# Expert weights in half-size transfers: eight half buffers, one per step, in place of four buffers of two steps

## The chip, the cores and the metric

The kernel runs on one core of one Trainium2 chip. The metric is device time in microseconds (us) of one execution. Everything is computed in float32. SBUF has 128 partitions; weights come from HBM by DMA over the core's 16 DMA engines.

## What is computed

The reference is two model blocks in a row on 256 tokens of width 1024. The first block has two layers, each a hybrid mixer (HGRN, attention, SSM) and then a PEER layer: for each token, 8 heads choose 16 of 16,384 experts each, and every expert is one row `down` and one row `up` of 1024 numbers. The second block has an RG-LRU layer and a sparse attention layer, each with an MLP.

Only the PEER layers are touched by the change. In short, with `h` the normed tokens:

```
scores  = top 16 of (sub_key_1 . q1 + sub_key_2 . q2)      per head
gate    = softmax(scores)
y[t]    = sum over chosen e of gate[t, e] * gelu(h[t] . down[e]) * up[e]
x       = x + y
```

## The kernel before, in words

The PEER layer splits the tokens. The first 160 (`DT_TOK`) go the dense way: TensorE computes `h . down[e]` for all experts, one step for each 128 experts, and later multiplies by all the `up` rows; non-chosen experts have a gate of zero. The other 96 tokens go the sparse way: GpSimd gathers the rows of their chosen experts (`PAIR`, 96 tiles of 128 rows, 8 KB a row, 1 MB a tile, four buffers, `GBUF`), and VectorE works them off, a dot product (`dot`, L1561) and a weighted sum (`weigh`, L1574) for each. GpSimd issues gather j when `weigh(j - 4)` is done (L975).

The dense way has 128 `hidden` steps (L740 to L750) and then 128 `back` steps (L766 to L777) on TensorE. One step multiplies eight 128x128 weight tiles, 512 KB, with the 160 tokens. Each float32 matmul is two instructions, so a step is 16 matmul instructions. In HBM two steps' weights lie side by side: a row of `experts` is 8 KB for a partition, 4 KB for each step (`pairs`, L1970).

SyncE brings the weights, one transfer of 1 MB for two steps (L362), into `ring`, four buffers of 8 KB a partition (`RING`, `buffer_of`). A buffer is handed back after its second step: by `hidden_ready` (one for each step, SyncE waits for every second one, L359) or by `step_used` (which TensorE raises after every odd `back` step, L776). SyncE issues in order, and TensorE waits for the buffer's semaphore `step_loaded` at each step. There are 128 such transfers in a layer, 256 in all.

Other work is laid by hand between the steps. 20 times in the second half of the `hidden` steps and 20 times in the first half of the `back` steps, after each third step, TensorE makes the gate matrices (`gates`, L762, 16 instructions); VectorE prepares the one-hots, multiplies the gates into the activations (`keep`, L1692) and then does `TILES_AT[n]` gather tiles. When the last `keep` is done, VectorE does the remaining tiles back to back while TensorE goes on with `back` steps from the 60th to the 128th. After step 120 TensorE waits until all 96 tiles are added (`pair_added`) and folds them in (L808, L809). At the end of each section SyncE clears the semaphores before the other engines go on (L380 to L382). Two MLPs use the same ring with transfers of their own (`stream`), which the change leaves alone.

Of the kernel before, what the change touches and what calls it, by code (L numbers as in the profile page):

```python
# [31 lines left out]
NKEYS = 128  # L32
# [4 lines left out]
RING = 4  # L37
# [23 lines left out]
PAIRS = NKEYS  # L61
# [4 lines left out]
def slot_of(section, b):  # L66
    return SLOT_ORDER[section][b % SLOTS]
# [6 lines left out]
    return earlier + b // SLOTS + 1  # L74


def buffer_of(layer, i):
    return (i + 2 * layer) % RING


class Chain:
# [17 lines left out]
def program(nc, I, out):  # L99
    ctx = ExitStack()  # L100
    with ctx:
        def sb(n, s, d=F32):
            return ctx.enter_context(nc.sbuf_tensor(n, s, d))

        ring = sb("weight_ring", [P, SLOTS * SLOT])
# [152 lines left out]
            "xs_turned xs_ready cum_rows decay_exponent decay_ready decayed_scores ssm_product z_silu ssm_mean ssm_root "  # L258
            "mix_turned mix_T key_scores scores_copied"
        ).split()  # L260
        stream_names = "step_loaded0 step_loaded1 step_loaded2 step_loaded3 step_used hidden_ready stream_added dve_chain".split()
        peer_names = (
            "gate_bent gate_exp_ready choice_ready choice_turned choice_T "
            "onehots_ready gates_product hidden_kept gated routing_done pack_ready "
# [9 lines left out]
        S = {n: ctx.enter_context(nc.semaphore(n)) for n in names}  # L274
# [29 lines left out]
        def _(sp):  # L304
            def block(n, b, load):

                s = slot_of(n, b)
                sp.dma_start(ring[:, s * SLOT:(s + 1) * SLOT], load(b)).then_inc(block_loaded[s], 16)
# [8 lines left out]
            def clear(group):  # L317
                for name in group:
                    sp.sem_clear(S[name])
# [30 lines left out]
            def peer(l, load, ahead):  # L350

                last_in_slot = {slot_of(l, b): b for b in range(HYBRID_BLOCKS)}
                for i in range(PAIRS):
                    r = buffer_of(l, i)
                    if i < RING:

                        sp.wait_ge(S["proj_done"], 2 * last_in_slot[r // 2] + 2)
                    elif i < PAIRS // 2 + RING:
                        sp.wait_ge(S["hidden_ready"], 2 * (i - RING + 1))  # L359
                    else:  # L360
                        sp.wait_ge(S["step_used"], i - RING + 1 - PAIRS // 2)
                    sp.dma_start(ring[:, r * 2048:(r + 1) * 2048], load(i)).then_inc(S[f"step_loaded{r}"], 16)  # L362
                    if i == PAIRS // 2 + 16:

                        sp.wait_ge(S["hidden_kept"], NKEYS + 2)
                        sp.wait_ge(S["gated"], GROUPS)
                        clear(front_names[:len(front_names) // 2])
                    if i == PAIRS // 2 + 20:
                        clear(front_names[len(front_names) // 2:])

                sp.wait_ge(S["gated"], 2 * GROUPS)
                for b in range(SLOTS):
                    if b:
                        sp.wait_ge(S["step_used"], PAIRS // 2 - 4 + 2 * b)
                    block(l + 1, b, ahead)

            def section_clear(n, group):
# [42 lines left out]
        def _(pe):  # L420
# [316 lines left out]
            def peer(l):  # L737
                gate_bank = lambda n: bank[(2, 3, 4)[n % 3] if n < GROUPS else (2, 3, 0)[n % 3]]

                def hidden(s):  # L740

                    i, r = s // 2, buffer_of(l, s // 2)
                    pe.wait_ge(S[f"step_loaded{r}"], 16 * (i // RING + 1))

                    pe.wait_ge(S["hidden_kept"], s + 1)
                    w = ring[:, r * 2048 + (s % 2) * 1024:r * 2048 + (s % 2 + 1) * 1024]
                    for k in range(KD):
                        last = mm(bank[s % 2][:, 0:DT_TOK], w[:, k * P:(k + 1) * P], HT[:, k, 0:DT_TOK],  # L748
                                  start=k == 0, stop=k == KD - 1)
                    last.then_inc(S["hidden_ready"], 1)  # L750

                def gates(n):

                    pe.wait_ge(S["onehots_ready"], n + 1)
                    if n >= 3:

                        pe.wait_ge(S["gated"], n - 2)
                    if n >= GROUPS:

                        pe.wait_ge(S["hidden_kept"], NKEYS + 2)  # L760
                    for j in range(8):
                        last = mm(gate_bank(n)[:, j * HALF:(j + 1) * HALF], OH1[:, n % 2, j, :], OH2[:, n % 2, j, :],  # L762
                                  start=True, stop=True)
                    last.then_inc(S["gates_product"], 1)

                def back(s):  # L766

                    i = NKEYS // 2 + s // 2
                    r = buffer_of(l, i)
                    pe.wait_ge(S[f"step_loaded{r}"], 16 * (i // RING + 1))  # L770
                    w = ring[:, r * 2048 + (s % 2) * 1024:r * 2048 + (s % 2 + 1) * 1024]
                    for k in range(KD):
                        last = mm(bank[4 + k // 2][:, (k % 2) * DT_TOK:(k % 2 + 1) * DT_TOK], w[:, k * P:(k + 1) * P], HACT[:, s, :],  # L773
                                  start=s == 0 and k % 2 == 0, stop=s == NKEYS - 1, skip_group_check=True)
                    if s % 2:
                        last.then_inc(S["step_used"], 1)  # L776
                    return last  # L777

                for s in range(CHOICE_AT):
                    hidden(s)  # L780
                pe.wait_ge(S["choice_ready"], 6)
                for w, src in enumerate((N1, N2, TS)):
                    turn(bank[2 + w][:, 0:P], src[:, 0, :, :].rearrange("p a b -> p (a b)"))
                    turn(bank[2 + w][:, P:DT_TOK], src[0:DT_TOK - P, 1, :, :].rearrange("p a b -> p (a b)"),
                         DT_TOK - P).then_inc(S["choice_turned"], 1)
                for s in range(CHOICE_AT, HALF):
                    hidden(s)
                n = 0
                for s in range(HALF, NKEYS):
                    hidden(s)  # L790
                    if s - HALF in HIDDEN_GATE_AT:
                        gates(n)
                        n += 1

                pe.wait_ge(S["gated"], GROUPS)
                for s in range(HALF):
                    back(s)
                    if s in GATE_AT:
                        gates(n)
                        n += 1  # L800
                pe.wait_ge(S["gated"], 2 * GROUPS)
                for s in range(HALF, NKEYS):
                    back(s)
                    if s == NKEYS - 8:

                        pe.wait_ge(S["pair_added"], TILES)
                        for q in range(2):
                            mm(bank[2 + q][GT0 - P:P, :], fold[:, 0:64], ACC[:, 0, q * 512:(q + 1) * 512], start=True, stop=True)  # L808
                            mm(bank[2 + q][GT1 - P:GT0 - P, :], fold[:, 64:96], ACC[:, 1, q * 512:(q + 1) * 512], start=True, stop=True)  # L809
                pe.wait_ge(S["step_used"], PAIRS // 2)  # L810
                pe.sem_inc(S["down_done"], 1)

                pe.wait_ge(S["down_copied"], 4)
                for k in range(KD):
                    last = turn(bank[k // 4][:, (k % 4) * P:(k % 4 + 1) * P], OT[:, k, 0:P])
                last.then_inc(S["back_turned"], 1)
                for k in range(KD):
                    last = turn(bank[2 + k // 4][0:DT_TOK - P, (k % 4) * P:(k % 4 + 1) * P], OT[:, k, P:DT_TOK])
                last.then_inc(S["back_turned"], 1)
# [11 lines left out]
            w = blk(3)  # L831
            for n in range(4):

                pe.wait_ge(S["conv_done"], n + 1)
                for j in range(2):
# [3 lines left out]
                    for g in range(2):  # L839
                        for k in range(2):  # L840
                            last = mm(bank[c % 4][:, g * T:(g + 1) * T],
                                      w[:, 2 * n + k, g * 256 + j * P:g * 256 + (j + 1) * P], XR[:, 2 * n + k, :],
                                      start=k == 0, stop=k == 1)
# [15 lines left out]
            for b in (3, 4):  # L859
                w = blk(b)  # L860
# [4 lines left out]
                for g in range(NG):  # L865

                    for half in range(2):
                        for k in range(KD):
                            last = mm(bank[4 + 2 * (b % 2) + g // 2][64 * half:64 * half + 64, (g % 2) * T:(g % 2 + 1) * T],  # L869
                                      w[:, k, g * HD:(g + 1) * HD], HT[:, k, :], start=k == 0, stop=k == KD - 1)  # L870
# [9 lines left out]
            for w in range(2):  # L880
                for r in range(32):
                    for half in range(2):
                        p0 = 64 * half
                        last = mm(bank[2 * w + half][0:64, 0:45].rearrange("p (c n) -> p c n", n=NC), w1[p0:p0 + 64, w, r, :],
                                  ZC[p0:p0 + 64, w, :, r:r + 16 * (NC - 1) + 1:16], start=r == 0, stop=r == 31)
# [8 lines left out]
            for x in range(4):  # L894
                last = mm(bank[5][0:NC, x * HD:(x + 1) * HD], HID[0:64, 1, x // 2, (x % 2) * NC:(x % 2 + 1) * NC], W2[0:64, 1, :],
                          start=True, stop=True)
# [1107 lines left out]
```

## Time and profile before

| | us |
|---|---|
| median of 3 runs | 2658.49 |
| lowest, highest | 2653.73, 2660.36 |
| the profiled execution, its own time | 2662.17 |
| its span | 2660.4 |
| TensorE busy in it | 2572.5 (97%) |
| VectorE busy in it | 1322.6 (50%) |

The profile's page gives busy time, then the span in 40 slices of 66.5 us. In the slices, one digit is the busy share in tenths. The two PEER layers' dense steps lie from 255 to 903 us and from 1143 to 1790 us. Times in the trace are from the span's start. "PE" is TensorE's matmul, "PEld" its weight load, "q1" the DMA queue of SyncE, "q0" that of GpSimd's gathers, "q10" that of ScalarE.

### The profile page before, as it was taken

The page shows a single profiled execution, that of the slowest core. Times are in us where ns is not written, and L with a number is a line of the kernel's source. Part 1 is how long each engine was busy: PE and PEld are TensorE (multiplying, and loading weights), DVE is VectorE, ACT ScalarE, POOL GpSimd, SP SyncE. Part 2 cuts the span into 40 slices and gives each one's busy share as a digit, 9 for nine tenths or more (in the row PEclk, how much of TensorE's full clock was granted, in tenths as well). Part 3 has the DMA queues.
Part 4 walks back from the last instruction along what each step waited for, and adds up shares of the span by engine and source line. Part 5 has one row for each costly group of instructions (what it writes and reads, how often), then busy time and mean ns, then how long its engine had stood idle before and what let it go on. Part 6 is the DMA issues. An engine that isn't in the chain of part 4 may idle for free.

```text
span 2660.4 us, 36834 instructions
## 1 busy us (share of the span) xinstructions
PE 2572.5 (97%) x15426; PEld 2167.1 (81%) x15426; DVE 1322.6 (50%) x2597; ACT 407.4 (15%) x1166; POOL 211.0 (8%) x208
## 2 busy tenths in 40 slices
PE   6999999999999999999999999999999999999998
PEld 5557999999999865699999999888666677776665
DVE  3843786888853185178687886414400010541001
ACT  2121121111110122022211111003100000430000
POOL 0000111222211000001121221100000000000000
PEclk9999999999999999999999999999999999889999
DMA  5213798999999532159899999973244442003442
GB/s 204 102 64 113 267 381 321 392 395 409 417 420 385 186 127 95 64 209 374 305 386 397 402 412 419 421 278 126 101 154 146 152 153 105 1 1 127 151 149 95
DMA packets 84758, 625.38 MB, mean 235 GB/s; under 512 B 10443, under 2 KB 12978, under 8 KB 14206
## 3 DMA queue, kind: packets, MB, share of 16 engines
q1 hardware_dynamic: 55580, 420.85, 41.3%
q0 software_dynamic: 28032, 201.54, 18.6%
q8 instruction: 113, 1.85, 0.3%
q10 hardware_dynamic: 994, 0.82, 0.1%
q14 instruction: 39, 0.32, 0.0%
HBM read 621.91 MB, written 1.06 MB: 234 GB/s over the span
## 4 chain that ended last, share of the span: by engine, by line
PE 86%; DVE 6%; DMA 5%; ACT 1%; issue 1%; SPq 0%; DVEq 0%; PEldq 0%; ACTq 0%
PE bank L748 17%; PE bank L773 17%; PE bank L499 9%; PE bank L513 8%; PE bank L521 8%; PE bank L762 5%; DMA weight_ring<-in_experts 5%; PE bank L464 4%; PE bank L476 3%; PE bank L869 2%; PE bank L426 1%; PE bank L918 1%; PE bank L488 1%; PE bank L430 1%; PE bank L937 1%
## 5 line engine op out<-in xcount | busy, mean ns | idle before, releaser
L773 PE MATMUL bank<-arena,weight_ring 128*128 128x160 f32 x4096 | 573.6, 301 | 10.7 <-DMA weight_ring<-in_experts 10.6
L773 PEld LDWEIGHTS bank<-arena,weight_ring 128*128 128x128 f32 x4096 | 558.6, 190 | 19.1 <-DMA weight_ring<-in_experts 17.4
L748 PE MATMUL bank<-hidden_T,weight_ring 128*128 128x160 f32 x4096 | 569.0, 301 | 5.1 <-ACT arena L1100 5.1
L748 PEld LDWEIGHTS bank<-hidden_T,weight_ring 128*128 128x128 f32 x4096 | 559.7, 191 | 6.1 <-issue 5.9
L1561 DVE CUSTOM_DVE_ANT_0 arena<-arena 128x1024 f32<-128x1024 f32 x192 | 234.7, 1222 | 168.4 <-DMA arena<-in_expert_rows,choice_by_pair 167.8
L976 POOL DMA_INDIRECT arena<-in_expert_rows,choice_by_pair x192 | 203.8, 1062 | 831.2 <-DVE arena L1574 786.3
L499 PE MATMUL bank<-hidden_T,weight_ring 128*128 128x256 f32 (+1 forms) x1088 | 241.9, 383 | 14.1 <-DMA weight_ring<-in_dense_h 7.4
L499 PEld LDWEIGHTS bank<-hidden_T,weight_ring 128*128 128x128 f32 (+1 forms) x1088 | 203.2, 188 | 47.1 <-issue 8.9
L1574 DVE SCALAR_TENSOR_TENSOR arena<-arena,pair_weights 128x1024 f32<-128x1024 f32 x188 | 240.8, 1281 | 0.2
L513 PEld LDWEIGHTS bank<-hidden_T,weight_ring 128*128 128x128 f32 x1024 | 195.0, 190 | 52.5 <-issue 29.6
L513 PE MATMUL bank<-hidden_T,weight_ring 128*128 128x256 f32 x1024 | 231.2, 380 | 0.0
L1718 DVE TENSOR_TENSOR weight_ring<-weight_ring 128x256 f32<-128x256 f32 x64 | 27.2, 425 | 409.1 <-ACT weight_ring L1146 409.1
L521 PE MATMUL bank<-weight_ring 128*128 128x512 f32 x512 | 229.9, 593 | 0.0
L521 PEld LDWEIGHTS bank<-weight_ring 128*128 128x128 f32 x512 | 97.5, 190 | 95.8 <-issue 92.6
L762 PE MATMUL bank<-weight_ring 128*128 128x64 f32 x1280 | 151.6, 272 | 0.0
L1100 ACT ACTIVATE arena<-bank 128x160 f32<-128x160 f32 x256 | 77.4, 303 | 484.3 <-PE bank L748 484.2
L762 PEld LDWEIGHTS bank<-weight_ring 128*128 128x128 f32 x1280 | 151.2, 192 | 0.0
L464 PE MATMUL bank<-weight_ring,hidden_T 128*128 128x512 f32 (+1 forms) x288 | 120.9, 574 | 0.0
L1106 ACT ACTIVATE pair_weights<-pair_dots 128x1 f32<-128x1 f32 x192 | 38.4, 200 | 508.3 <-DVE pair_dots L1561 508.2
L1680 DVE TENSOR_TENSOR weight_ring<-iota_row,weight_ring 128x1024 f32<-128x1024 f32 x80 | 97.5, 1219 | 8.9 <-ACT weight_ring L1122 8.9
L464 PEld LDWEIGHTS bank<-weight_ring,hidden_T 128*128 128x128 f32 x288 | 52.2, 195 | 57.0 <-issue 56.6
L1692 DVE TENSOR_TENSOR arena<-arena,bank 128x512 f32<-128x512 f32 x80 | 54.8, 685 | 78.5 <-PE bank L762 78.5
(320 smaller groups left out, 2007.4 us busy)
## 6 DMA issues: line engine op xcount, KB each, us to landing
weight_ring<-in_experts SPq DMA_DIRECT2D x256, 1024.0 KB, 8.9
weight_ring<-in_mlp SPq DMA_DIRECT2D x64, 1024.0 KB, 4.8
weight_ring<-in_dense_h SPq DMA_DIRECT2D x22, 2048.0 KB, 7.7
weight_ring<-in_dense_nsa SPq DMA_DIRECT2D x9, 2048.0 KB, 7.7
weight_ring<-in_dense_rg SPq DMA_DIRECT2D x7, 2048.0 KB, 7.9
arena<-in_expert_rows,choice_by_pair POOLq DMA_INDIRECT x192, 10.9
arena<-distance_bias_scratch SPq DMA_DIRECT2D x2, 768.0 KB, 5.7
residual<-in_x SPq DMA_DIRECT2D x1, 1024.0 KB
```

Source lines behind the costliest of these rows:

```text
L464: last = mm(bank[4 + 2 * (b % 2) + tt][:, 0:n], src[:, k, tt * P:(tt + 1) * P], w[:, k, 0:n], start=k == 0, stop=k == KD - 1)
L476: last = mm(bank[4 + 2 * ((first + c) % 2) + tt][:], HT[:, k, tt * P:(tt + 1) * P], w[c][:, k, :], start=k == 0, stop=k == KD - 1)
L499: last = mm(bank[4 + 2 * (b % 2) + j // 2][0:m, (j % 2) * T:(j % 2 + 1) * T], w[:, k, j * P:j * P + m], HT[:, k, :], start=k == 0, stop=k ...
L513: last = mm(bank[r % 2][:, 0:T], ring[:, r * 2048 + k * P:r * 2048 + (k + 1) * P], HT[:, k, :], start=k == 0, stop=k == KD - 1)
L521: last = mm(outs[o][:], act_c[:, r, (o // 2) * P:(o // 2 + 1) * P], ring[:, r * 2048 + 1024 + (o % 2) * 512:r * 2048 + 1024 + (o % 2 + 1) ...
L748: last = mm(bank[s % 2][:, 0:DT_TOK], w[:, k * P:(k + 1) * P], HT[:, k, 0:DT_TOK], start=k == 0, stop=k == KD - 1)
L762: last = mm(gate_bank(n)[:, j * HALF:(j + 1) * HALF], OH1[:, n % 2, j, :], OH2[:, n % 2, j, :], start=True, stop=True)
L773: last = mm(bank[4 + k // 2][:, (k % 2) * DT_TOK:(k % 2 + 1) * DT_TOK], w[:, k * P:(k + 1) * P], HACT[:, s, :], start=s == 0 and k % 2 == ...
L976: pool.indirect_dma_start(PAIR[:, j % GBUF, :], None, I["expert_rows"], bass.IndirectOffsetOnAxis(ap=picked[:, 0, j:j + 1].bitcast(U32), a ...
L1561: V.tensor_tensor_reduce(out=rows, in0=rows, in1=GX[:, j // TILES0, :], scale=1.0, scalar=0.0, op0=ALU.mult, op1=ALU.add, accum_out=adot[: ...
L1574: V.scalar_tensor_tensor(acc, rows, c, acc, ALU.mult, ALU.add).then_inc(S["pair_added"], 1)
L1680: V.tensor_tensor(OH1[:, n % 2, :, :], bc(iota[:].unsqueeze(1), [P, 8, P]), bc(it[:, 0], [P, 8, P]), ALU.is_equal)
```

## The change

Each 1 MB transfer becomes two of 512 KB, one for each step. The ring becomes eight half buffers of 4 KB a partition (`half_of`), each with its own semaphore; the memory is the same. The source of a transfer is one half of the 8 KB row, so a partition gets 4 KB in one piece. Each half is handed back by its own step: SyncE waits for every single `hidden_ready`, and TensorE raises `step_used` after every `back` step. SyncE issues 256 transfers in a layer in place of 128. The section clears have four semaphores more. The places where SyncE clears names between the transfers and where it begins the next section's blocks are the same, counted in steps. Matmuls, VectorE, ScalarE and GpSimd are unchanged.

```diff
-def buffer_of(layer, i):
-    return (i + 2 * layer) % RING
+def half_of(layer, h):
+    return (h + 4 * layer) % (2 * RING)
...
-                for i in range(PAIRS):
-                    r = buffer_of(l, i)
-                    if i < RING:
-
-                        sp.wait_ge(S["proj_done"], 2 * last_in_slot[r // 2] + 2)
-                    elif i < PAIRS // 2 + RING:
-                        sp.wait_ge(S["hidden_ready"], 2 * (i - RING + 1))
+                for h in range(2 * PAIRS):
+                    r = half_of(l, h)
+                    if h < 2 * RING:
+
+                        sp.wait_ge(S["proj_done"], 2 * last_in_slot[r // 4] + 2)
+                    elif h < NKEYS + 2 * RING:
+                        sp.wait_ge(S["hidden_ready"], h - 2 * RING + 1)
                     else:
-                        sp.wait_ge(S["step_used"], i - RING + 1 - PAIRS // 2)
-                    sp.dma_start(ring[:, r * 2048:(r + 1) * 2048], load(i)).then_inc(S[f"step_loaded{r}"], 16)
-                    if i == PAIRS // 2 + 16:
+                        sp.wait_ge(S["step_used"], h - 2 * RING + 1 - NKEYS)
+                    sp.dma_start(ring[:, r * 1024:(r + 1) * 1024], load(h // 2)[:, (h % 2) * 1024:(h % 2 + 1) * 1024]).then_inc(
+                        S[f"step_loaded{r}"], 16)
+                    if h == NKEYS + 32:
...
                 def back(s):
 
-                    i = NKEYS // 2 + s // 2
-                    r = buffer_of(l, i)
-                    pe.wait_ge(S[f"step_loaded{r}"], 16 * (i // RING + 1))
-                    w = ring[:, r * 2048 + (s % 2) * 1024:r * 2048 + (s % 2 + 1) * 1024]
+                    r = half_of(l, NKEYS + s)
+                    pe.wait_ge(S[f"step_loaded{r}"], 16 * ((NKEYS + s) // (2 * RING) + 1))
+                    w = ring[:, r * 1024:(r + 1) * 1024]
...
-                    if s % 2:
-                        last.then_inc(S["step_used"], 1)
+                    last.then_inc(S["step_used"], 1)
```

## Rows read from the trace of the kernel before

**Rows 1.** The page, part 2: the span in 40 slices.

```profile
PE   6999999999999999999999999999999999999998
DMA  5213798999999532159899999973244442003442
```

**Rows 2.** Stretches, both layers: columns as the second line names them.

```profile
core 0: us, PE busy (x) PEld busy (x) DVE busy (x) ACT busy (x) POOL busy (x), PEclk, DMA share, GB/s
580.00:739.00 159.00, 159.00 (x1229) 159.00 (x1228) 134.30 (x173) 16.41 (x66) 35.09 (x33) 1.00 1.01 411
739.00:846.00 107.00, 101.86 (x723) 98.25 (x722) 53.26 (x68) 10.95 (x44) 18.73 (x20) 1.00 1.01 420
846.00:883.00 37.00, 37.00 (x272) 36.89 (x272) 3.52 (x4) 0.50 (x2) 0.00 (x0) 1.00 0.73 263
```

**Rows 3.** Groups by line, 739 to 846 us, then PEld from 1626 to 1740 us.

```profile
L773 PEld LDWEIGHTS bank<-arena,weight_ring 128*128 128x128 f32 x721 | 98.4, 190 | 8.8 <-DMA weight_ring<-in_experts 8.8
L1561 DVE CUSTOM_DVE_ANT_0 arena<-arena 128x1024 f32<-128x1024 f32 x23 | 28.2, 1226 | 56.3 <-DMA arena<-in_expert_rows,choice_by_pair 56.3
L1574 DVE SCALAR_TENSOR_TENSOR arena<-arena,pair_weights 128x1024 f32<-128x1024 f32 x22 | 28.2, 1281 | 0.0
...
L773 PEld LDWEIGHTS bank<-arena,weight_ring 128*128 128x128 f32 x771 | 105.1, 190 | 8.7 <-DMA weight_ring<-in_experts 8.7
```

**Rows 4.** Timeline: start us, us, what, idle before.

```profile
796.05 1.23 DVE L1561 CUSTOM_DVE_ANT_0 arena<-arena 128x1024 f32<-128x1024 f32 x1 [2.53 <-DMA arena<-in_expert_rows,choice_by_pair]
796.11 4.37 PEld L773 LDWEIGHTS bank<-arena,weight_ring 128*128 128x128 f32 x32 [0.57 <-DMA weight_ring<-in_experts]
...
798.75 0.94 POOL L976 DMA_INDIRECT arena<-in_expert_rows,choice_by_pair  x1 [4.02 <-DVE arena L1574]
801.02 1.23 DVE L1561 CUSTOM_DVE_ANT_0 arena<-arena 128x1024 f32<-128x1024 f32 x1 [2.54 <-DMA arena<-in_expert_rows,choice_by_pair]
801.09 4.37 PEld L773 LDWEIGHTS bank<-arena,weight_ring 128*128 128x128 f32 x32 [0.61 <-DMA weight_ring<-in_experts]
```

**Rows 5.** DMA by queue (packets, MB, share), 739 to 846 us, and issues to landing.

```profile
q1 hardware_dynamic: 3123, 22.78, 51.1%
q0 software_dynamic: 3045, 22.12, 49.8%
...
weight_ring<-in_experts SPq DMA_DIRECT2D x23, 1024.0 KB, 14.9
arena<-in_expert_rows,choice_by_pair POOLq DMA_INDIRECT x20, 12.2
```

**Rows 6.** The same view, 580 to 739 us.

```profile
weight_ring<-in_experts SPq DMA_DIRECT2D x28, 1024.0 KB, 9.3
arena<-in_expert_rows,choice_by_pair POOLq DMA_INDIRECT x33, 10.6
```

**Rows 7.** DMA by queue in the start-up: 5.0 to 5.5, then 6.5 to 7.0 us.

```profile
q10 hardware_dynamic: 29, 0.06, 70.3%
q1 hardware_dynamic: 29, 0.04, 28.1%
...
q10 hardware_dynamic: 57, 0.10, 51.8%
q1 hardware_dynamic: 58, 0.03, 19.6%
```

**Rows 8.** DMA by queue, 2657 to 2659 us: the output alone.

```profile
q1 hardware_dynamic: 199, 0.82, 101.9%
```

**Rows 9.** Landing, 260 to 335 us (L976), and SyncE's issues, 739 to 846 us.

```profile
DMA to landing us min/median/max: 5.9/11.8/17.3
...
L362 SPq DMA_DIRECT2D weight_ring<-in_experts x23: 327/328/328, 741.4 to 845.6; - x23
```

**Rows 10.** Timeline at the section's end, and the chain's first `hidden` steps.

```profile
909.04 1.13 PE L430 MATMUL bank<-identity 128*128 128x128 f32 x8 [3.49 <-SPq L382]
...
255.42 82.80 PE bank L748 x608
```

**Rows 11.** A stretch in which TensorE often stands, just after the section's end.

```profile
903.00:912.00 9.00, 4.93 (x42) 4.59 (x43) 3.40 (x9) 3.35 (x7) 0.00 (x0) 1.00 0.84 281
20.00:40.00 20.00, 12.62 (x64) 11.02 (x63) 4.87 (x9) 1.17 (x3) 0.00 (x0) 0.83 0.94 355
```

More of the change, by code:

```diff
@@ L260, in program @@
         ).split()
-        stream_names = "step_loaded0 step_loaded1 step_loaded2 step_loaded3 step_used hidden_ready stream_added dve_chain".split()
+        stream_names = "step_loaded0 step_loaded1 step_loaded2 step_loaded3 step_loaded4 step_loaded5 step_loaded6 step_loaded7 step_used hidden_ready stream_added dve_chain".split()
         peer_names = (
@@ L367, in peer @@
                         clear(front_names[:len(front_names) // 2])
-                    if i == PAIRS // 2 + 20:
+                    if h == NKEYS + 40:
                         clear(front_names[len(front_names) // 2:])
@@ L373, in peer @@
                     if b:
-                        sp.wait_ge(S["step_used"], PAIRS // 2 - 4 + 2 * b)
+                        sp.wait_ge(S["step_used"], NKEYS - 8 + 4 * b)
                     block(l + 1, b, ahead)
@@ L740, in hidden @@
                 def hidden(s):
-                    i, r = s // 2, buffer_of(l, s // 2)
-                    pe.wait_ge(S[f"step_loaded{r}"], 16 * (i // RING + 1))
+                    r = half_of(l, s)
+                    pe.wait_ge(S[f"step_loaded{r}"], 16 * (s // (2 * RING) + 1))
                     pe.wait_ge(S["hidden_kept"], s + 1)
-                    w = ring[:, r * 2048 + (s % 2) * 1024:r * 2048 + (s % 2 + 1) * 1024]
+                    w = ring[:, r * 1024:(r + 1) * 1024]
                     for k in range(KD):
@@ L766, in back @@
                 def back(s):
-                    i = NKEYS // 2 + s // 2
-                    r = buffer_of(l, i)
-                    pe.wait_ge(S[f"step_loaded{r}"], 16 * (i // RING + 1))
-                    w = ring[:, r * 2048 + (s % 2) * 1024:r * 2048 + (s % 2 + 1) * 1024]
+                    r = half_of(l, NKEYS + s)
+                    pe.wait_ge(S[f"step_loaded{r}"], 16 * ((NKEYS + s) // (2 * RING) + 1))
+                    w = ring[:, r * 1024:(r + 1) * 1024]
                     for k in range(KD):
@@ L809, in peer @@
                             mm(bank[2 + q][GT1 - P:GT0 - P, :], fold[:, 64:96], ACC[:, 1, q * 512:(q + 1) * 512], start=True, stop=True)
-                pe.wait_ge(S["step_used"], PAIRS // 2)
+                pe.wait_ge(S["step_used"], NKEYS)
                 pe.sem_inc(S["down_done"], 1)
```

## The prediction, made before the change was run

> **What bounds the kernel now.** I read the slices first: TensorE is busy nearly everywhere, and DMA is at nine tenths or more in two long stretches, the PEER layers [rows 1]. So TensorE sets the time, and DMA is the resource that can stop it. Then the PEER layer by stretches: while gates are made (580 to 739 us) TensorE never stands, though DMA runs at 411 GB/s; from 739 to 846 us its weight loads are busy 98.25 of 107 us, at 420 GB/s; after 846 us it is full again and DMA has room [rows 2]. The groups say what is missing: 8.8 us of idle time before the weight loads of L773 for want of `in_experts`, and 8.7 us in the other layer [rows 3]. These 17.5 us are all that better weight delivery could give. TensorE needs 82.80 / 38 = 2.18 us for a step of 512 KB (608 instructions are 38 steps) [rows 10], so it wants 240 GB/s.
>
> Why only there? In this tail VectorE takes gather tiles back to back. It works 1.23 + 1.28 = 2.51 us on one and would take 417 GB/s by itself; it waits 56.3 us for gathers [rows 3]. Both streams are hungry, and the timeline shows what comes of it: a tile and a pair of steps start every 4.97 us, in step with each other (796.05 to 801.02, 796.11 to 801.09) [rows 4]. In 4.97 us one transfer of 1 MB of each kind lands: 210 GB/s each, 22.78 against 22.12 MB [rows 5]. A step then comes every 2.49 us where 2.18 are wanted.
>
> **How the two queues share.** The whole case hangs on this. Weights take 14.9 us to land and gathers 12.2 [rows 5], so 14.9 / 4.97 = 3.0 weight transfers and 2.5 gathers are under way. Yet both get the same bandwidth. A single line served in order of arrival would give weights 3.0 of 5.5 parts and both the same delay. So each queue gets a turn, whatever waits behind it. What is a turn: a piece (the packet of the rows, one partition's run) or an equal amount of bytes? In the tail it can't be seen, since all pieces are 8 KB. The start-up shows two queues with unequal pieces: 29 packets against 29, then 57 against 58, while the bytes are 0.10 against 0.03 MB [rows 7]. The turn went by packets there. I take it to hold here too.
>
> The Trainium skill ("DMA: Bandwidth & Descriptors", Queues, rings and completion order) says that each DMA engine goes round its queues a packet at a time, a packet being some 9 to 17 descriptors. The start-up's equal counts agree with turns; how many pieces make one isn't shown by any row. By this rule a turn would be about one transfer's share of an engine, 32 KB against 64 KB after the change, which is the same one to two.
>
> **The change, part by part.**
>
> *Half-size pieces.* A weight piece is now 4 KB and a gather piece still 8 KB. Of 1 MB, an engine gets 8 pieces, so an 8 KB piece takes 4.97 / 16 = 0.311 us. A 4 KB piece took 2.0 x 16 x 1.019 / 199 = 0.164 us when the output was stored [rows 8]; it is a store, but the nearest row. The bounds are 0.156 (half of 0.311) and 0.18 (a guess at 10% worse than the row). A turn of both is 0.475 us, eight make a half transfer and a gather tile: 3.80 us each. So in the tail a step comes every 3.80 us in place of 2.49, and a tile every 3.80 in place of 4.97.
>
> Would the gathers keep their queue filled at that pace? From the start of `dot` (796.05) to the next issue (798.75) are 2.7 us [rows 4]. The fastest gather took 5.9 us to land [rows 9], of which 2.5 are its own bytes at full rate; so 3.4 us are fixed, and with 3.8 of bytes the loop is 9.9 us for three tiles, 3.3 each. That is below 3.80: they keep it filled.
>
> *The tail, for one layer.* The gathers moved 22.12 MB, 21.1 tiles, from 739 to 846 us [rows 5]. Served faster before 739 us they would have a shorter queue by some 0.6 tile, so I take 20.5 tiles, 20.5 x 3.80 = 78 us: they are done near 817 us. TensorE could do 78 / 2.18 = 35.8 steps in that time. The queue brings 20.5, plus what lies landed at the start. How much? Before, TensorE wanted 107 / 2.18 = 49.1 steps and lost 8.8 us, 4.0 steps: 45.1 done, where 22.78 MB are 43.4. So 1.7 steps of stock counted. Halves add about one (handed back half a pair earlier, waited for half a pair less). Against that go the 0.6 tile of bytes that gathers have ahead of weights (1.2 steps), and the gate stretch, next. I take 1, between 0 and 2.7. Lost: 35.8 - 20.5 - 1 = 14.3 steps, 31.2 us, where 8.8 were lost before: +22.4 us. After the gathers end, a half lands in 8 x 0.164 = 1.31 us, and TensorE runs free as it does now from 846 us [rows 2]. There is no wait at step 120 now or then, as tiles end earlier, so finishing them early gives nothing back.
>
> *The gate stretch (580 to 739 us).* Three steps and one set of gates take 8.31 us with 1.8 tiles. DMA needs 24 x 0.311 / 2 = 3.73 us for the weights and 1.8 x 2.49 = 4.48 for the gathers now, 8.21 in all; with 4 KB pieces 24 x 0.164 = 3.94, 8.42 in all. So it falls behind by 0.11 us in each of 20 rounds, 2.2 us, which the buffers cover: landing takes 9.3 us [rows 6], 3.4 of the ring's steps at 2.77 us, and 3.6 lie landed. It costs the tail's stock up to 1.6 steps, nothing by itself. With 0.18 us pieces it would fall behind by 0.5 us a round, 10 us, and then TensorE stands here too.
>
> *Earlier hand-back.* It is worth the one step above, 2.2 us a layer, and only where a step waits for weights. In all `hidden` steps and after the tail weights wait for TensorE, so it is worth nothing there.
>
> *Issues and waits.* SyncE issues 256 more transfers at 0.328 us [rows 9], 84 us on an engine that has 2.18 us for each; hidden. TensorE has the same waits; 128 more increments ride on matmuls, nothing. If SyncE were late, a half would be issued under a microsecond later with seven others ahead. Four more semaphores are cleared at three section ends: the clear of 28 names is inside a wait of 3.49 us [rows 10], so four cost 0 to 0.5 us; 0.27 each, 0.8 in all.
>
> *TensorE's clock.* In the tail it would stand 1.6 of 3.8 us. From 903 to 912 us it was busy 4.93 of 9 us at a granted 1.00; from 20 to 40 us, after longer idling, at 0.83, so part of it at the lower of its levels [rows 11]. At 1.2 GHz a step would need 4.36 us, 0.56 more than the weights' pace; 0 to 10 us for both layers. I take 0, since it stands in short gaps.
>
> Sum: 2 x 22.4 + 0.8 = 45.6. The profiled execution took 2662.17 us (span 2660.4), 3.7 above the median of 2658.49. 2662.2 + 45.6 = 2707.8, and in terms of the median **2704 us**. With a stock of 2.7 steps and gathers at 4.2 us each it is +30; with none, slow pieces and some low clock +62: 2688 to 2720 for this case.
>
> **Rivals.**
>
> *Equal bytes.* A turn could be worth the same bytes whatever the piece (two 4 KB pieces for one of 8 KB). Then the share stays half, the tail stays at 2.49 us a step, and only the earlier hand-back counts: 2 x -2.2 + 0.8 = -3.6, 2655 us. For it: the equal shares of the tail fit as well [rows 5]. Against it: the start-up's counts [rows 7], though its pieces are all 4 KB or less. The Trainium skill (same page, SWDGE vs HWDGE vs iDMA) wants a packet to be 4096 B at most, as the boundary at which an engine changes over; if an 8 KB piece were cut so, this rival would follow.
>
> *The stalls go: not slower, faster.* If what is under way counted after all, seven halves (3.5 MB) against 2.5 gathers would give weights 58% of 420 GB/s, 245, just over the 240 wanted. The 17.5 us go: 2658.5 - 17.5 + 0.8 = 2642 us. It decides at a share of 57%. Against it: today 55% under way gets 51% [rows 5].
>
> *Starved earlier.* The pieces cost 10% more than the output's, the gate stretch stands too, or the clock falls for long: above 2720.
>
> **How the numbers follow.** Turns by piece 0.72, equal bytes 0.18, stalls gone 0.06, starved earlier 0.04. The predicted time is that of the first. With 0.76 between 2688 and 2720 or above, the range must take in most of the equal-bytes case to hold 8 in 10: 2652 to 2722. A measurement of this kernel tells about 0.3% (8 us) from no change. Slower by more: 0.76. Within: most of equal bytes, 0.16. Faster: 0.08.
>
> **What would show it.** In the profile after: from 739 us on, packets of q1 and q0 nearly alike but bytes one to two; steps every 3.8 us; tiles every 3.8 us and the last near 817 us, not 846; idle before L773's weight loads some 30 us a layer. If equal bytes hold, tiles still come every 5 us and that idle is some 6 to 7 us. The prediction is wrong if q1 keeps 22 MB in the tail, or if the gathers' latency rather than their share sets their pace. TensorE's 159 of 159 us in the gate stretch should stay; if it doesn't, the stock was overrated.

## The result, and the profile after

The changed kernel takes 2690.5 us in the median, where the kernel before took 2656.6 us beside it: a ratio of 1.0128, 95% interval 1.0109 to 1.0148. The profiled execution took 2691.34 us, 29.2 more than the profiled one of before. Below, the ratio behind each measured time is again to the kernel before, timed beside it, with its 95% interval.

The page gives the span and SyncE's queue (packets, MB, share of 16 engines). The same bytes now go in 92,444 packets; before it was 55,580 for 420.85 MB.

```profile
span 2689.5 us, 37102 instructions
...
q1 hardware_dynamic: 92444, 420.86, 42.2%
```

The groups by line, whole run, then the tails of the two layers alone (739 to 826 us, 1640 to 1760 us); they answer to [rows 3]:

```profile
L773 PEld LDWEIGHTS bank<-arena,weight_ring 128*128 128x128 f32 x4096 | 558.8, 190 | 49.8 <-DMA weight_ring<-in_experts 48.0
...
L773 PEld LDWEIGHTS bank<-arena,weight_ring 128*128 128x128 f32 x462 | 63.3, 190 | 23.9 <-DMA weight_ring<-in_experts 23.9
...
L773 PEld LDWEIGHTS bank<-arena,weight_ring 128*128 128x128 f32 x703 | 96.0, 190 | 24.2 <-DMA weight_ring<-in_experts 24.1
```

The weight loads wait 48.0 us for DMA, 24 in each layer, where it was 8.8 and 8.7. The 30.5 us more are about the difference of the two executions (29.2), and all of it lies in the tails: the gate stretch still has no idle time.

The timeline answers to [rows 4]:

```profile
757.03 2.20 PEld L773 LDWEIGHTS bank<-arena,weight_ring 128*128 128x128 f32 x16 [0.21 <-DMA weight_ring<-in_experts]
760.79 2.20 PEld L773 LDWEIGHTS bank<-arena,weight_ring 128*128 128x128 f32 x16 [1.56 <-DMA weight_ring<-in_experts]
764.54 2.20 PEld L773 LDWEIGHTS bank<-arena,weight_ring 128*128 128x128 f32 x16 [1.55 <-DMA weight_ring<-in_experts]
...
783.35 2.20 PEld L773 LDWEIGHTS bank<-arena,weight_ring 128*128 128x128 f32 x16 [1.57 <-DMA weight_ring<-in_experts]
785.88 2.20 PEld L773 LDWEIGHTS bank<-arena,weight_ring 128*128 128x128 f32 x16 [0.33 <-DMA weight_ring<-in_experts]
```

A step comes every 3.76 us, and once in a while one after 2.5 us. The gather tiles run in the same beat, but about one in seven comes only after 5.1 us:

```profile
770.29 1.23 DVE L1560 CUSTOM_DVE_ANT_0 arena<-arena 128x1024 f32<-128x1024 f32 x1 [1.37 <-DMA arena<-in_expert_rows,choice_by_pair]
774.02 1.22 DVE L1560 CUSTOM_DVE_ANT_0 arena<-arena 128x1024 f32<-128x1024 f32 x1 [1.30 <-DMA arena<-in_expert_rows,choice_by_pair]
779.16 1.23 DVE L1560 CUSTOM_DVE_ANT_0 arena<-arena 128x1024 f32<-128x1024 f32 x1 [2.71 <-DMA arena<-in_expert_rows,choice_by_pair]
...
822.08 1.23 DVE L1560 CUSTOM_DVE_ANT_0 arena<-arena 128x1024 f32<-128x1024 f32 x1 [1.33 <-DMA arena<-in_expert_rows,choice_by_pair]
```

The DMA queues from 739 to 820 us, for [rows 5] (packets, MB, share):

```profile
q0 software_dynamic: 2905, 21.18, 63.0%
q1 hardware_dynamic: 3427, 12.48, 38.5%
```

The bytes are 12.5 against 21.2 MB: the share of the weights fell from a half to 37%. The weights sent 18% more packets than the gathers over the whole tail. Two short stretches show why (774 to 779 us, then 783 to 787 us):

```profile
q0 software_dynamic: 184, 1.38, 66.6%
q1 hardware_dynamic: 186, 0.67, 33.4%
...
q1 hardware_dynamic: 253, 0.94, 58.4%
q0 software_dynamic: 103, 0.71, 43.1%
```

In the first the counts are equal and the bytes one to two. In the second the weights sent nearly twice as many, which turns allow only where the gathers' queue had run empty. Such a stretch came 4 to 5 us after the start of each late tile (from 760, 783 and 811 us on).

The trace also has the start and the length of every single packet, and so shows the turns themselves. In the kernel before, from 760 to 840 us, a weight piece starts within the 5 ns before the end of a gather piece in 89% of the cases, and a gather piece before the end of a weight piece in 86%. For two pieces of the same queue it is 10% and 9%, no more than by chance (some 11%). So the two queues took turns by single pieces.

Last the stretches (columns as in [rows 2]):

```profile
720.00:740.00 20.00, 20.00 (x156) 20.00 (x156) 15.09 (x21) 1.99 (x8) 4.50 (x4) 1.00 1.02 415
760.00:780.00 20.00, 12.62 (x83) 11.42 (x84) 11.90 (x16) 2.48 (x10) 4.70 (x5) 1.00 1.02 416
840.00:860.00 20.00, 20.00 (x149) 20.00 (x148) 0.00 (x0) 0.00 (x0) 0.00 (x0) 1.00 0.74 244
```

TensorE is busy 12.6 of 20 us in the tail and full on both sides of it, and the granted clock stays at 1.00, the higher of its two levels.

### The profile page after: what moved, and what is told of

The parts are those of the page before. It is cut to its first block, busy times and chain, and to the rows that moved or that the text cites. A ratio compares the mean times of both kernels' runs of the same rounds, so it can differ in the third digit from the quotient of the medians.

```text
span 2689.5 us, 37102 instructions
## 1 busy us (share of the span) xinstructions
PE 2570.7 (96%) x15426; PEld 2163.1 (80%) x15426; DVE 1322.5 (49%) x2597; ACT 407.5 (15%) x1166; POOL 215.0 (8%) x208
## 3 DMA queue, kind: packets, MB, share of 16 engines
q1 hardware_dynamic: 92444, 420.86, 42.2%
## 4 chain that ended last, share of the span: by engine, by line
PE 85%; DVE 6%; DMA 6%; ACT 1%; issue 1%; SPq 0%; DVEq 0%; another core or an unknown queue 0%; PEldq 0%; ACTq 0%
PE bank L773 17%; PE bank L749 17%; PE bank L500 9%; PE bank L514 8%; PE bank L522 8%; PE bank L763 5%; DMA weight_ring<-in_experts 5%; PE bank L465 3%; PE bank L477 3%; PE bank L868 2%; PE bank L427 1%; PE bank L431 1%; PE bank L917 1%; PE bank L489 1%; PE bank L936 1%
## 5 line engine op out<-in xcount | busy, mean ns | idle before, releaser
L773 PE MATMUL bank<-arena,weight_ring 128*128 128x160 f32 x4096 | 576.0, 301 | 39.1 <-DMA weight_ring<-in_experts 38.8
L773 PEld LDWEIGHTS bank<-arena,weight_ring 128*128 128x128 f32 x4096 | 558.8, 190 | 49.8 <-DMA weight_ring<-in_experts 48.0
```

## The experiments

**Which of the three is it: the pieces, the size of the transfers, or the hand-back?** The change does all three at once. The first two kernels do one alone.

*One 1 MB transfer for two steps, handed back by pairs, in 4 KB pieces.*

```diff
-sp.dma_start(ring[:, r * 2048:(r + 1) * 2048], load(i)) ...
+sp.dma_start(ring[:, 0:8192].rearrange("p (h b n) -> p h b n", h=2, b=RING)[:, :, r, :],
+             load(i).rearrange("p (h n) -> p h n", h=2)) ...
```

The cut code has two more waits, since a buffer now lies in two places: the first transfers of a layer wait for the last blocks of both slots, and the next section's second and third block for the last step.

> The kernel before, with each 1 MB transfer kept whole and handed back by pairs, but its two steps put 16 KB apart in a partition, so that its pieces are 4 KB (the next section's second and third block are asked for only when all steps are done). Theory (turns go by piece): the weights' bytes in the tail fall to one third, as in the changed kernel; without the earlier hand-back it is 2 to 4 us worse than that one, 2690 to 2700 us. Rival (turns by transfer, or equal bytes): as before, 2655 to 2662 us.

Measured: 2696.4 us, 1.0135 (1.0108 to 1.0162). The queues from 739 to 820 us:

```profile
q0 software_dynamic: 2852, 20.74, 61.7%
q1 hardware_dynamic: 3352, 12.93, 39.8%
```

This is the changed kernel's picture with none of its other parts. Piece size alone makes the loss; turns by whole transfers and equal bytes both fall. It came out 6 us over the changed kernel, the side on which the missing early hand-back was expected (the two were timed in separate comparisons, and 6 us is little more than their spread). The traces point the same way: from the first dense step to the fold a layer takes 645.6 and 647.8 us here, 643.6 and 643.2 in the changed kernel.

*Two 512 KB transfers in 8 KB pieces.*

```diff
-sp.dma_start(ring[:, r * 2048:(r + 1) * 2048], load(i)) ...
+for q in range(2):
+    sp.dma_start(ring[64 * q:64 * q + 64, r * 2048:(r + 1) * 2048], load(i)[64 * q:64 * q + 64, :]) ...
```

> The kernel before, with each 1 MB transfer issued as two of 512 KB by partitions (0 to 63, then 64 to 127): the count and the size of the transfers are those of the changed kernel, but every piece keeps its 8 KB, and the buffers and the hand-back stay as before. Theory (turns go by piece, piece size is the cause): the tail shares stay 1:1, a step every 2.49 us, idle before the weight loads of L773 about 9 us a layer, time as before, 2654 to 2661 us. Rival (turns go by transfer, so half-size transfers are the cause): an engine gets 4 pieces of weights a turn against 8 of gathers, share one third, a step every 3.7 us or more in the tail, 2685 to 2700 us. Rival (more issues and more semaphore work are the cause): also about 2690 us.

Measured: 3265.7 us, 1.2253 (1.2194 to 1.2312), far outside what any theory said. Weights alone, 262 to 300 us, then both streams, 700 to 1000 us:

```profile
DMA packets 1268, 8.32 MB, mean 219 GB/s; under 512 B 254, under 2 KB 254, under 8 KB 254
...
DMA packets 10881, 75.35 MB, mean 251 GB/s; under 512 B 1695, under 2 KB 1695, under 8 KB 1695
...
q0 software_dynamic: 5409, 39.37, 53.4%
q1 hardware_dynamic: 5459, 35.78, 47.9%
```

Transfers to 64 of the partitions moved 219 GB/s alone, with the engines busy all the time; in the changed kernel the weights, alone from 822 to 830 us and to all 128 partitions, moved 405. As a test of the total it decides nothing. Its shares still say something: packets 5459 to 5409 and bytes nearly alike, though each weight transfer brings an engine half as many pieces as a gather does. Turns by transfer would have given one to two.

**The other side of the same scale: smaller gather pieces.** If turns go by piece, cutting the gathers should undo the change.

```diff
-pool.indirect_dma_start(PAIR[:, j % GBUF, :], None, I["expert_rows"], ...)
+for q, rows in enumerate(("rows_down", "rows_up")):
+    pool.indirect_dma_start(PAIR[:, j % GBUF, q * D:(q + 1) * D], None, I[rows], ...)
```

> The changed kernel, with each gather of 8 KB rows split into two of 4 KB rows (down and up from tables of their own), so that both queues have 4 KB pieces. Theory (turns go by piece): shares go back to 1:1; both at about 205 GB/s, a step every 2.6 us in the tail, idle before the weight loads 7 to 13 us a layer, 2655 to 2668 us. Rival (the queue of 512 KB transfers is slow by itself, or the hand-back costs): stays at 2690 us.

Measured: 2669.6 us, 1.0041 (1.0024 to 1.0058): most of the loss is gone. The queues from 785 to 845 us:

```profile
q0 software_dynamic: 3364, 12.26, 51.2%
q1 hardware_dynamic: 3364, 12.23, 51.1%
```

and the timeline of the weight loads there:

```profile
801.39 2.20 PEld L773 LDWEIGHTS bank<-arena,weight_ring 128*128 128x128 f32 x16 [0.37 <-DMA weight_ring<-in_experts]
803.94 2.20 PEld L773 LDWEIGHTS bank<-arena,weight_ring 128*128 128x128 f32 x16 [0.35 <-DMA weight_ring<-in_experts]
```

3364 packets each, equal bytes, a step every 2.56 us (2.6 was expected). The idle for weights is 18.1 us for both layers, against 17.4 in the kernel before. So what the change had cost in the tail is gone; the 11 us that are left lie elsewhere. TensorE stands 13.5 us among the `hidden` steps where the changed kernel has 6.5 (the next experiment shows the place), and 1.5 us before one set of gates.

*The same cut of the gathers in the kernel before.*

> The kernel before (8 KB weight pieces), with each gather split into two of 4 KB rows. Theory (turns go by piece): weights may take up to two thirds, more than the 240 GB/s that TensorE wants, so the 17.5 us of idle before the weight loads go; gathers come every 5.8 us or so in the tail and end near step 120; 2638 to 2650 us. Rival (equal bytes, or shares that follow what is under way): the tail stays as it is, 2655 to 2662 us, or slower by GpSimd's doubled issues.

Measured: 2659.5 us, 1.0009 (0.9989 to 1.0029), a miss. The idle for weights did go, as the theory says; the gain did not come. Where it went can be read in the timeline (a stop among the first `hidden` steps of each layer, then the weight loads in the tail and the fold):

```profile
333.72 56.63 PEld L748 LDWEIGHTS bank<-hidden_T,weight_ring 128*128 128x128 f32 x416 [3.54 <-issue]
1213.10 37.07 PEld L748 LDWEIGHTS bank<-hidden_T,weight_ring 128*128 128x128 f32 x261 [4.53 <-issue]
...
741.44 134.78 PEld L773 LDWEIGHTS bank<-arena,weight_ring 128*128 128x128 f32 x992
878.64 0.19 PEld L808 LDWEIGHTS bank<-arena,fold_parts 128*64 128x64 f32 x2 [2.42 <-DVE arena L1575]
```

In the tail there are 62 steps without a gap, then a wait for the tiles before the fold, 2.4 us here and 7.3 in the other layer. The other loss is far from the tail. Just after the first gathers are issued (from 321.8 and 1201.2 us), TensorE stands 3.5 and 4.5 us among the `hidden` steps, which the kernel before does not; in all, its weight loads of L748 idle 14.0 us in place of 5.9. ScalarE, whose results these steps wait for, stands 5.4 and 7.6 us just then, and the profile names no engine that it waits for. So 17.4 us of idle went, and 9.7 at the fold and 8.1 among the `hidden` steps came. Why ScalarE stands there is open. Both kernels with all gathers cut have this stop, and the next one does not.

*So the cut only where the weights starve, for the last 20 gathers.*

```diff
+TAIL = TILES - 20
...
+if j < TAIL:
+    pool.indirect_dma_start(PAIR[:, j % GBUF, :], None, I["expert_rows"], ...)
+    continue
+for q, rows in enumerate(("rows_down", "rows_up")):
+    pool.indirect_dma_start(PAIR[:, j % GBUF, q * D:(q + 1) * D], None, I[rows], ...)
```

> The kernel before (8 KB weight pieces); only the last 20 gathers of each layer are split into two of 4 KB rows, so the gate stretch keeps its whole gathers. Theory (turns go by piece, and what weights gain the gathers lose): no idle before the weight loads; about 411 - 240 = 171 GB/s are left for gathers, a tile every 6 us, the last near 870 us against step 120 at 874 us, so the wait at step 120 is 0 to 4 us a layer; 2640 to 2648 us, faster than the kernel before by 9 to 17 us. Rival (splitting gathers costs by itself): 2655 us or more, with the weight loads idle or GpSimd late.

Measured: 2641.9 us, 0.9928 (0.9911 to 0.9944), within what was expected. No idle for weights; the last tile starts at 869.78 us and the fold does not wait:

```profile
869.78 1.23 DVE L1568 CUSTOM_DVE_ANT_0 arena<-arena 128x1024 f32<-128x1024 f32 x1 [3.81 <-DMA arena<-in_rows_up,choice_by_pair]
873.84 0.19 PEld L809 LDWEIGHTS bank<-arena,fold_parts 128*64 128x64 f32 x2 [0.17 <-DVE arena L1581]
```

**Do half buffers cost anything without the gathers beside them?** In this pair of kernels the last 20 gathers of each layer are left out, and VectorE works on old rows in their place.

```diff
-for j in range(TILES):
+for j in range(TILES - 20):
```

> The changed kernel with the last 20 gathers of each layer left out (VectorE works on old rows, so its output is not the reference's). Weights are then alone in the tail. Theory (halves cost only by their share against the gathers): no idle before the weight loads, about 17 us under the kernel before, 2640 to 2645 us, and the same as its counterpart without halves within 3 us. Rival (hand-back by step, twice the issues, or 4 KB pieces cost by themselves): 10 us or more above the counterpart.

> The kernel before with the last 20 gathers of each layer left out in the same way. All theories: no idle before the weight loads, 2638 to 2645 us.

Measured: 2640.2 us (0.9933, 0.9916 to 0.9950) with halves and 2640.5 us (0.9939, 0.9919 to 0.9960) without. In both the idle of L773's weight loads for DMA is gone. Twice the issues, twice the increments and 4 KB pieces cost nothing that shows; early hand-back brings nothing either when nobody waits.

**Is it the share alone, or how much is under way?** The last 20 gathers are issued one tile later.

```diff
-pool.wait_ge(S["pair_added"], j - GBUF + 1)
+pool.wait_ge(S["pair_added"], j - GBUF + 1 + (j >= TILES - 20))
```

> The changed kernel; the last 20 gathers of each layer are issued one tile later (two under way in place of three). Theory (each queue gets a turn while it has something waiting): the gathers' queue runs empty part of the time, tiles come every 4.9 us or so in place of 3.8, weights get the rest; idle before the weight loads falls from 24 to some 10 us a layer, 2660 to 2670 us, though the tail of tiles ends later (near 840 us). Rival (share fixed by piece size whenever both streams run): idle stays about 24 us or grows with the longer tail, 2690 us or more.

Measured: 2640.2 us, 0.9930 (0.9913 to 0.9947). Better than expected: the idle is gone wholly, 50 us below the changed kernel and 16 below the kernel before. The queues and the landings (745 to 840 us), then the group of the gather tiles (745 to 846 us):

```profile
q1 hardware_dynamic: 6177, 22.49, 59.1%
q0 software_dynamic: 2296, 16.70, 42.5%
...
weight_ring<-in_experts SPq DMA_DIRECT2D x44, 512.0 KB, 10.6
arena<-in_expert_rows,choice_by_pair POOLq DMA_INDIRECT x16, 8.8
```

```profile
L1560 DVE CUSTOM_DVE_ANT_0 arena<-arena 128x1024 f32<-128x1024 f32 x18 | 22.1, 1225 | 57.7 <-DMA arena<-in_expert_rows,choice_by_pair 57.7
```

Weights get 22.49 MB in 95 us, 237 GB/s, and gathers the rest. So a piece size sets the share only while both queues have something waiting. A gather now lands after 8.8 us with two under way; so a tile comes every (8.8 + 2.7) / 2 = 5.7 us. I had expected 4.9, with a landing of 7.2.

*The same delay in the kernel before.*

> The kernel before with the same delay of the last 20 gathers. Theory: tiles every 5.5 us, weights get the 240 GB/s that TensorE wants, idle before the weight loads falls from 8.8 to 0 to 2 us a layer, tiles end near 850 us, still ahead of step 120; 2640 to 2647 us, faster than the kernel before. Rival (the shares of the tail are 1:1 whatever is under way): 2655 to 2662 us.

Measured: 2655.7 us, 0.9998 (0.9984 to 1.0012), a miss of the same kind as above. The weight loads do not wait, but (the last tile, and the fold):

```profile
881.39 1.23 DVE L1561 CUSTOM_DVE_ANT_0 arena<-arena 128x1024 f32<-128x1024 f32 x1 [3.65 <-DMA arena<-in_expert_rows,choice_by_pair]
885.26 0.29 PEld L808 LDWEIGHTS bank<-arena,fold_parts 128*64 128x64 f32 x2 [9.45 <-DVE arena L1574]
```

Here a gather lands after 10.4 us, beside 8 KB pieces in place of 4 KB ones; a tile takes 6.6 us (5.5 was expected), the last starts at 881.4 us, and TensorE waits 9.5 us at step 120, and 9.8 in the other layer. With halves the last tile starts at 867.1 us, ahead of it. The gain went into a new wait at another place.

*Moving the fold from after step 120 to after step 127*, first with that delay, then by itself, then in the changed kernel with the delay:

```diff
-if s == NKEYS - 8:
+if s == NKEYS - 1:
```

> The kernel before with the last 20 gathers issued one tile later, and the fold of the sparse tiles moved from after step 120 to after step 127. Theory (the delay took the wait from the weights to the tiles at step 120, and nothing else): TensorE waits for neither, tiles end near 885 us, before step 127 ends; 2638 to 2645 us. Rival (something else of the delayed gathers cost the gain): 2655 us.

> The kernel before with the fold of the sparse tiles moved from after step 120 to after step 127, and nothing else. Theory (in the kernel before only the weights' share costs, the fold's place hides at most the copy behind the last step, 1 to 2 us a layer): idle before the weight loads stays 17 us, 2652 to 2658 us. Rival (the move alone made most of the gain of before_tail3_fold_last): 2636 to 2645 us.

> The changed kernel with the last 20 gathers issued one tile later and the fold moved to after step 127. Theory (halves are neutral once the weights' share is enough): the same as before_tail3_fold_last within 4 us, 2633 to 2640 us. Rival (halves cost or gain by themselves): 5 us or more apart from it.

Measured: 2635.3 us (0.9915, 0.9898 to 0.9931), 2656.0 us (0.9989, 0.9977 to 1.0001) and 2639.6 us (0.9917, 0.9895 to 0.9938). The first has the fold at 889.31 us after the last tile at 881.59, with 0.17 us of wait:

```profile
881.59 1.23 DVE L1561 CUSTOM_DVE_ANT_0 arena<-arena 128x1024 f32<-128x1024 f32 x1 [4.46 <-DMA arena<-in_expert_rows,choice_by_pair]
889.31 0.19 PEld L808 LDWEIGHTS bank<-arena,fold_parts 128*64 128x64 f32 x2 [0.17 <-issue]
```

The move alone gives nothing that can be told from noise. With it and the delay, whole buffers and half buffers have ratios of 0.9915 and 0.9917: with enough bandwidth, no difference between the two ways of buffering shows. Both beat the kernel before and the changed one.

## Why the prediction was right, step by step

It said 2704 us, 45.6 us more in the profiled execution; 29.2 came. The direction, the place and the mechanism held; the tail's added loss was sized almost half too high (22.4 us a layer in place of 15.3). Its lower case (a stock of 2.7 steps, gathers at 4.2 us each) was put at +30 and comes close, though how that sum follows from its terms is not shown. The range, 2652 to 2722 us, held the equal-bytes case too, so it is the packet counts and not the time that tell the mechanisms apart.

*Turns by piece*: held. The profile after has equal packets with unequal bytes, and both one-sided experiments (4 KB weight pieces alone, gather pieces cut to match) moved the shares as it says. The prediction took this from 29 packets in the start-up and said that the tail can't show it; the starts of single packets in the tail of the kernel before show it directly. The equal-bytes rival falls with `one_transfer_4k`. The rival of the stalls gone falls as a forecast, but its price was right: 2642 us said, 2640 to 2642 in the four kernels in which neither weights nor tiles kept TensorE waiting and the fold stayed in its place.

*A turn of 0.475 us, so 3.80 us for a step and a tile*: 3.76 was measured. The price of a 4 KB piece, taken from a store, held for the loads: 0.162 us in the median in the changed kernel from 774 to 779 us. But one tile in about seven took 5.1 us: 21 tiles from 738.78 to 822.08 us are 3.97 each. After such a gap the weights get an extra half.

*They keep their queue filled*: this step failed. From 783 to 787 us the gathers moved 0.71 MB and the weights 0.94, so the gathers' queue had run empty. I took 9.9 us for three tiles, from a landing of 3.4 + 3.8 us. With 8.8 us of landing as in `after_tail3` it would be 2.7 + 8.8 = 11.5, just over 3 x 3.8 = 11.4: an estimate that puts the gathers at the edge. Why a tile in seven is late was not shown.

*The tail*: expected to last 78 us with 35.8 steps wanted, 20.5 brought and 1 in stock, 14.3 lost. The end at 822.5 us makes it 83.5 us and 38.3 steps wanted. 23.9 us of idle are 11.0 steps, so 27.3 were done. The queue brought 12.48 MB in 81 us, 24.5 steps in 83.5. The stock was thus 2.8, the upper end I had named. The two terms I had taken from it, the gathers' shorter queue and the lag of the gate stretch, did not show. Loss a layer: 24 us in place of 31.2, so +15.3 in place of +22.4; twice 7.1 us is nearly the whole miss of 16.4. Of the 3.3 steps a layer that make it, 1.8 are the stock, put at 1 for want of a measured value. The other 1.5 are the queue: 4.0 more steps brought, less 2.5 more wanted in the longer tail.

*The gate stretch*: TensorE stays full, as said. *Issues, waits, clock*: nothing that shows, as said; the pair without tail gathers shows it for all of them together, and the clock was granted in full at 63% busy. *Clears*: priced at 0.8 us. The waits of TensorE at the ends of the two layers are 3.97 and 3.24 us, where they were 3.75 and 2.65, 0.8 more in all.

*Earlier hand-back*: priced at 2.2 us a layer. `one_transfer_4k` against the changed kernel fits with 3 a layer, and their traces with 2.0 and 4.6, but the spread of the times is as large; unresolved.

The Trainium skill ("DMA: Bandwidth & Descriptors", Queues, rings and completion order) has engines change queues at packets of some 9 to 17 descriptors. The turns agree; the length does not, and here the measurement decides. A turn as long as one transfer's share does not fit the equal bytes of `two_transfers_8k` (35.78 against 39.37 MB), and in the tail of the kernel before the other queue follows after a single piece (89% and 86% of the cases, above).

## What to carry to other kernels

When two DMA queues are both kept waiting, compare the size of their pieces (one partition's contiguous run), not of their transfers: halving the run halved the stream's turn in bytes, and it was the stream that TensorE waited for. Before splitting a transfer, look whether another queue is saturated beside it; without it the split was free here. And when a stream is given more, look for who gets less and when he is due: the cured wait of 17 us came back as 19 us at the fold of the sparse tiles in one kernel, and as 10 us there and 8 among the `hidden` steps in another.

## What the hardware showed that was not expected

Transfers to 64 partitions (0 to 63, then 64 to 127, all 16 engines busy) moved 219 GB/s alone, and 251 GB/s together with the gathers beside them. In the kernel before, the same 8 KB pieces in transfers to 128 partitions moved 420 GB/s together with the gathers in the tail. The kernel took 3266 us for it. Why is open; no run looked into it.

How much is under way decides sharply near the edge: one gather fewer in the changed kernel took its idle from 24 us a layer to none.
